# Projection stage: which engine empties PSUM into the scaled key and q tiles, the value pieces and the value rows

## The chip, the cores and the metric

The kernel runs on one core of a Trainium2 chip. The metric is the time of one execution on the device, in microseconds. Three runs of the kernel before gave 1306.35, 1302.48 and 1300.43 us, the median being 1302.48 us.

The engines are named as in the profile: PE is TensorE, DVE is VectorE, ACT is ScalarE, POOL is GpSimd, SP is the engine that issues the DMAs. PEld is the loading of weights into TensorE.

## The reference, cut to what matters

Two transformer-like layers with 256 tokens and 1024 columns come first, and a third block of another kind follows. Each of the first two layers projects the normalised input, and works on q, keys and values like this:

```python
proj = h @ w_in
q = proj[..., o0:o1].reshape(B, S, NSA_HEADS, HEAD_DIM)          # 8 heads of 64
kv = proj[..., o1:o2].reshape(B, S, 2, N_BRANCH, KV_GROUPS, HEAD_DIM)
q = rope(rms_norm(q, q_norm), pos)
k_s = rope(rms_norm(k_all[:, :, 1], k_norm[1]), pos)             # selected branch
k_w = rope(rms_norm(k_all[:, :, 2], k_norm[2]), pos)             # window branch
k_cmp = compress(k_all[:, :, 0], cmp_pe[0], cmp_w1[0], cmp_w2[0], blk)
v_cmp = compress(v_all[:, :, 0], cmp_pe[1], cmp_w1[1], cmp_w2[1], blk)
s = einsum(q, k) * scale                                          # scale = 1/8
# rms_norm(x, g) = x * rsqrt(mean(x*x) + EPS) * g
```

After that come softmax attention over three branches, a pooling mixer, an output projection and a feed-forward part.

## The kernel before, in words

Everything is written out by hand: one program per engine, ordered by semaphores. Each engine takes its instructions strictly in order, so the order of the lines in `pe_layer`, `act_layer` and `dve_layer` is the order of the work.

**Weights.** They arrive as panels of 1 MB (`raw`). For nearly full precision a panel is split in two: ACT rounds it into `w_hi` (`split_hi`, L409), DVE takes the rest into `ring_w` (`split_lo`, L414), and PE does three products for each tile (`mm3`, L419 to L421). SP loads the panels, and between them the modulation weights (`load_mod`, L348), each when its buffer is free.

**Modulation.** DVE also computes the vector-matrix products of the modulation, as multiply-adds over 128x512 tiles (`dve_mod`, L1115 for the first and L1117 for the others). These pieces are placed between its other work, as `mod(0)`, `mod(1)` and so on. `mod(3)` takes four L1117 instructions and needs the modulation weights that SP issued when `mod(1)` was done.

**Projection stage** (twice, once for each layer). PE fills banks 4 and 5 in turn, and a bank may be written again when `gfree` of that bank says that it has been emptied. The panels are, in order: K0K1, K2V0, V1V2, Q0, CMP (the hidden layer of the compression), then the gate columns, Q1, U0, U1. `turn(j)` on PE (L571 and L573) multiplies the squares of two tiles of keys or q by a block matrix of ones (the sums of squares) and the scaled tile `ybuf[j]` by a rotation matrix. For each j the rest is shared: ACT computes the reciprocal root in `roots(j)` (L953, L955), POOL multiplies `ybuf[j]` by the cosines (L429), DVE multiplies the rotated tile in PSUM by the sines (L1181), adds POOL's product (L1186) and multiplies by the root (L1188). The result goes to `kr` or `qr`. ACT copies it into the stacked operands (L1010, L979), and DVE computes what the copies rounded away (L1289, L1196). PE's first score products (`pe_maxima`, L828) wait for the last of these (`st_lo`, L824). The next thing that PE waits for is `cmp_y` (L655), set by DVE behind the gates and the compressed keys (L1302, L1303).

**What the change touches.** In the kernel before, DVE writes these tiles out of PSUM:

- `ybuf[0]`, the scaled keys, in two halves (L1247, L1262), 128x256 each;
- the V pieces of the compression, `tb`, in four parts (L1256), 64x240 each; ACT writes the K pieces (L962);
- the value rows `vt` (L1271), 128x512;
- `ybuf[1]` and `ybuf[2]`, the scaled q tiles (`scaled`, L1169), 128x512, multiplied by the norm's gain and by 0.125.

Of the kernel before, what the change touches and what calls it, by code (L numbers as in the profile page):

```python
# [9 lines left out]
ALU = mybir.AluOpType  # L10
ACT = mybir.ActivationFunctionType
# [4 lines left out]
T = 256  # L16
TT = T // P
# [3 lines left out]
EPS = 1e-6  # L21
# [17 lines left out]

C_ID, C_BD, C_ROT, C_ONE, C_COS, C_SIN, C_CCOS, C_CSIN, C_CAUS, C_CMPM, C_VALID, C_EPS, C_LEPS, C_MF, C_MB, C_SG, C_NM, C_RC, C_RM, CN = (  # L40
    0, 128, 256, 384, 512, 768, 1024, 1040, 1056, 1184, 1216, 1217, 1218, 1219, 1347, 1475, 1476, 1477, 2501, 2503)
N_CMP = (T - 32) // 16 + 1
# [19 lines left out]
def constants():  # L62
# [20 lines left out]
    c[:, C_EPS] = EPS  # L83
    c[:, C_LEPS] = LN_EPS
    c[:, C_MF:C_MF + P] = np.where(p > f, NEG, 0.0)
    c[:, C_MB:C_MB + P] = np.where(f > p, NEG, 0.0)
# [9 lines left out]
def build(nc, a, out, layers=DEPTH):  # L96
# [8 lines left out]
    with ctx:  # L105
# [299 lines left out]
        def split_hi(act, m, k):  # L405

            landed(act, m, k)
            act.wait_ge(split_free, 4 * m + k + 1)
            nc.scalar.activation(w_hi[slot(k)][:, :], w_raw(m, k), ACT.Copy).then_inc(hi_done, 1)  # L409

        def split_lo(dve, m, k):

            dve.wait_ge(hi_done, 4 * m + k + 1)
            nc.vector.tensor_tensor(w_lo(m, k), w_raw(m, k), w_hi[slot(k)][:, :].bitcast(F32),  # L414
                                    ALU.subtract).then_inc(lo_done, 1)
# [519 lines left out]
        def act_layer(act, l, link, ahead):  # L935
# [11 lines left out]
            def roots(j):  # L947


                act.wait_ge(nr_mm, 4 * l + (1, 2, 4)[j])  # L950
                i = (0, 2, 6)[j]
                v = tbuf[:, 2 * j:2 * j + 2, :]
                nc.scalar.activation(v, two(bank[i % 4][:, :]), ACT.Ln, bias=cst[:, C_EPS:C_EPS + 1], scale=1.0 / 64).then_inc(ring_a, 1)  # L953
                ring_taken(act, l, i)
                nc.scalar.activation(v, v, ACT.Exp, scale=-0.5).then_inc(nr_rs, 1)  # L955
# [3 lines left out]
            for g in range(2):  # L959
                for j2 in range(2):  # L960
                    src = win(G(0), 64 * g, 64, [[2, 16], [16, 15]], j2)
                    last = nc.scalar.activation(tb[64 * j2:64 * j2 + 64, :, 15 * g:15 * g + 15], src, ACT.Copy)  # L962
            last.then_inc(tb_k, 1)
            split_hi(act, m, 4)
            used(L_K2V0)
            nc.scalar.activation(tbuf[:, 1, :], G(1)[:, 0:T], ACT.Square).then_inc(nr_sq, 1)

            act.wait_ge(tb_pe, l + 1)
            nc.scalar.activation(tbh[:, :, :], tb, ACT.Copy).then_inc(tb_hi, 1)
            split_hi(act, m, 5)  # L970
            split_hi(act, m, 6)

            def stack(bp):
# [21 lines left out]
            used(L_Q0)  # L995
            nc.scalar.activation(tbuf[:, 2:4, :], two(G(3)[:, :]), ACT.Square).then_inc(nr_sq, 1)
            used(L_CMP)
            nc.scalar.activation(ce, bank[6][:, 0:60], ACT.Exp, scale=-1.0).then_inc(cmp_e, 1)
# [16 lines left out]
            used(L_Q1)  # L1015
            nc.scalar.activation(tbuf[:, 4:6, :], two(G(5)[:, :]), ACT.Square).then_inc(nr_sq, 1)
            act.wait_ge(nr_mm, 4 * l + 3)
            link(nc.scalar.activation(sqc[:, 16:31], bank[6][:, 256:271], ACT.Ln, bias=cst[:, C_EPS:C_EPS + 1], scale=1.0 / 64))
# [131 lines left out]
        def dve_layer(dve, l, link, ahead):  # L1150
# [13 lines left out]

            def scaled(j):


                dve.wait_ge(nr_sq, 5 * l + (3, 5)[j - 1])
                nc.vector.tensor_scalar(ybuf[j], two(G((3, 5)[j - 1])[:, :]), lc[:, LC_QN:LC_QN + 1], 0.125, ALU.mult, ALU.mult).then_inc(gfree[1], 1)  # L1169

            def rotated(j, parts=(0, 1)):
# [72 lines left out]

            used(L_K0K1)
            dve.wait_ge(tb_k, l + 1)
            nc.vector.tensor_scalar(ybuf[0][:, 0, :], G(0)[:, T:2 * T], lc[:, LC_KN + 1:LC_KN + 2], None, ALU.mult).then_inc(gfree[0], 1)  # L1247

            split_lo(dve, m, 4)
            used(L_K2V0)  # L1250

            dve.wait_ge(nr_sq, 5 * l + 2)
            for g in range(2):
                for j2 in range(2):
                    src = win(G(1), 64 * g, 64, [[2, 16], [16, 15]], T + j2)
                    last = nc.vector.tensor_copy(tb[64 * j2:64 * j2 + 64, :, 30 + 15 * g:45 + 15 * g], src)  # L1256
            last.then_inc(tb_v, 1)
            dve.wait_ge(tb_v, l + 1)
            pe_bc = win(lc, 0, P, [[2, 16], [1, 2], [0, 30]], LC_PE)
            tb4 = tb.rearrange("p j (v n) -> p j v n", v=2)  # L1260
            nc.vector.tensor_tensor(tb4, tb4, pe_bc, ALU.add).then_inc(tb_pe, 1)
            nc.vector.tensor_scalar(ybuf[0][:, 1, :], G(1)[:, 0:T], lc[:, LC_KN + 2:LC_KN + 3], None, ALU.mult).then_inc(gfree[1], 1)  # L1262
            nc.vector.memset(vt[:, :, :, 64:65], 1.0)
# [5 lines left out]
            split_lo(dve, m, 5)  # L1269
            used(L_V1V2)  # L1270
            nc.vector.tensor_copy(vt[:, :, :, 0:64], G(2)[:, :].rearrange("p (t s d) -> p t s d", t=TT, s=4)).then_inc(gfree[0], 1)  # L1271
            mod(1)
            split_lo(dve, m, 6)
            mod(2)

            scaled(1)
            dve.wait_ge(cmp_e, l + 1)
# [26 lines left out]
            split_lo(dve, m, 7)  # L1304
            scaled(2)
            maxima(0, (0, 1))
# [1145 lines left out]
```

## Time and profile before

| | |
|---|---|
| median of three runs | 1302.48 us |
| the profiled execution, own time | 1304.12 us |
| its span, first to last instruction | 1302.1 us |
| PE busy | 1214.6 us, 93% |
| DVE busy | 939.3 us, 72% |
| ACT busy | 608.3 us, 47% |
| chain that ended last | PE 70%, DVE 17%, DMA 7%, issue 3%, ACT 3% |
| mean granted clock of TensorE | 0.965 |

The span leaves out 2.0 us of the profiled execution's own time. "PEclk" is the clock that TensorE was granted, 1.00 being the level of 2.4 GHz and 0.5 that of 1.2 GHz. "Idle before" in square brackets is the time for which the engine stood still before an instruction, and which engine released it; "issue" means that the profile shows nobody for it. Starts are counted from the start of the span. The first layer's projection stage lies at about 46 to 112 us and the second layer's at about 388 to 454 us. Consecutive instructions of an engine overlap a little in the records, so that the distance between two starts says more than the duration.

### The profile page before, as it was taken

The numbers are of one execution on the slowest core, as the hardware profiler recorded it, in microseconds if no ns is written. First come the engines' busy times: TensorE is split into PE (matmuls) and PEld (weight loads), VectorE is DVE, ScalarE is ACT, GpSimd is POOL, SyncE is SP. The second block draws the span as 40 slices with busy tenths as digits, with TensorE's granted clock in tenths as the row PEclk, the third lists the DMA queues.
The fourth block names the chain that finished last, engine by engine and source line by source line (L and its number), as shares of the span: only waits on it lengthen the run. The fifth ranks groups of instructions, "written<-read, shape, count | busy, mean of one in ns | idle before, by whom it ended". The sixth has DMA issues, their size and how long they took to land.

```text
span 1302.1 us, 20323 instructions
## 1 busy us (share of the span) xinstructions
PE 1214.6 (93%) x8294; PEld 1103.9 (85%) x8294; DVE 939.3 (72%) x1211; ACT 608.3 (47%) x796; POOL 48.3 (4%) x54
## 2 busy tenths in 40 slices
PE   6799999999989999999999999998789999999996
PEld 5778889899889779899998998887669998788885
DVE  5798797786898986855657559987784647765565
ACT  2444344344344542544444435469685743444441
POOL 1003100000000140000000000000000000000000
PEclk7699999999999999999999999899989999999999
DMA  9772266667766422645556533255753463455540
GB/s 371 283 271 87 105 266 230 251 228 270 276 245 230 181 102 98 237 166 191 194 177 228 201 140 122 98 178 178 242 212 130 162 250 139 169 188 192 193 161 33
DMA packets 43804, 249.87 MB, mean 192 GB/s; under 512 B 4208, under 2 KB 12416, under 8 KB 15568
## 3 DMA queue, kind: packets, MB, share of 16 engines
q1 hardware_dynamic: 43280, 246.66, 52.0%
q0 software_dynamic: 448, 2.12, 0.4%
q8 instruction: 56, 0.92, 0.3%
q14 instruction: 20, 0.16, 0.0%
HBM read 247.66 MB, written 1.11 MB: 191 GB/s over the span
## 4 chain that ended last, share of the span: by engine, by line
PE 70%; DVE 17%; DMA 7%; issue 3%; ACT 3%; SPq 0%; DVEq 0%; ACTq 0%
PE bank L419 14%; PE bank L420 14%; PE bank L421 14%; PE bank L770 11%; DMA arena<-in_modw 5%; PE bank L771 5%; DVE ring_w L414 3%; DVE macc L1117 3%; PE bank L859 2%; DVE arena L1117 2%; DVE arena L2051 1%; PE bank L900 1%; DMA arena<-dscr 1%; PE bank L541 1%; PE bank L752 1%
## 5 line engine op out<-in xcount | busy, mean ns | idle before, releaser
L414 DVE TENSOR_TENSOR ring_w<-raw,w_hi 128x2048 fp32r<-128x2048 f32 x170 | 389.6, 2294 | 157.6 <-ACT w_hi L409 157.0
L409 ACT ACTIVATE w_hi<-raw 128x2048 fp32r<-128x2048 f32 x170 | 323.9, 1909 | 140.1 <-PE bank L421 121.5
L770 PE MATMUL bank<-act,w_hi 128*128 128x512 f32 x736 | 262.0, 398 | 6.2 <-DVE arena L1419 6.0
L419 PE MATMUL bank<-act,w_hi 128*128 128x256 f32 x800 | 237.3, 297 | 8.4 <-DVE act L1147 7.0
L420 PE MATMUL bank<-act,w_hi 128*128 128x256 f32 x800 | 231.1, 289 | 0.0
L421 PE MATMUL bank<-act,ring_w 128*128 128x256 f32 x800 | 230.9, 289 | 0.0
L771 PE MATMUL bank<-act,ring_w 128*128 128x256 f32 x736 | 206.2, 280 | 0.0
L419 PEld LDWEIGHTS bank<-act,w_hi 128*128 128x128 f32 x800 | 158.5, 198 | 17.0 <-issue 16.8
L770 PEld LDWEIGHTS bank<-act,w_hi 128*128 128x128 f32 x736 | 138.4, 188 | 39.6 <-DVE arena L1419 7.2
L419 PE MATMUL bank<-ff_hi,w_hi 128*128 128x256 f32 (+1 forms) x560 | 158.5, 283 | 1.0 <-issue 1.0
L420 PE MATMUL bank<-ff_lo,w_hi 128*128 128x256 f32 (+1 forms) x560 | 158.8, 283 | 0.0
L420 PEld LDWEIGHTS bank<-act,w_hi 128*128 128x128 f32 x800 | 158.6, 198 | 0.1
L421 PE MATMUL bank<-ff_hi,ring_w 128*128 128x256 f32 (+1 forms) x560 | 158.7, 283 | 0.0
L421 PEld LDWEIGHTS bank<-act,ring_w 128*128 128x128 f32 x800 | 158.3, 198 | 0.0
L771 PEld LDWEIGHTS bank<-act,ring_w 128*128 128x128 f32 x736 | 139.2, 189 | 0.5
L419 PEld LDWEIGHTS bank<-ff_hi,w_hi 128*128 128x128 f32 x560 | 107.4, 192 | 2.4 <-issue 1.1
L1068 ACT ACTIVATE arena<-bank 128x256 f32<-128x256 f32 x96 | 36.6, 383 | 154.7 <-PE bank L771 150.1
L421 PEld LDWEIGHTS bank<-ff_hi,ring_w 128*128 128x128 f32 x560 | 107.5, 192 | 0.0
L420 PEld LDWEIGHTS bank<-ff_lo,w_hi 128*128 128x128 f32 x560 | 107.5, 192 | 0.0
L1117 DVE SCALAR_TENSOR_TENSOR macc<-arena,cact,macc 128x512 f32<-128x512 f32 x105 | 82.5, 785 | 3.3
L1419 DVE TENSOR_TENSOR arena<-bank,arena 128x256 f32<-128x256 f32 x96 | 38.5, 419 | 45.9 <-ACT arena L1068 45.9
L1075 ACT ACTIVATE ff_hi<-arena 128x512 fp32r<-128x512 f32 x48 | 30.0, 626 | 64.6 <-DVE arena L1422 64.6
(337 smaller groups left out, 1957.5 us busy)
## 6 DMA issues: line engine op xcount, KB each, us to landing
raw<-in_panels SPq DMA_DIRECT2D x170, 1024.0 KB, 4.9
arena<-in_modw SPq DMA_DIRECT2D x48, 1024.0 KB, 6.7
mixf<-dscr SPq DMA_DIRECT2D x8, 512.0 KB, 4.4
arena<-dscr SPq DMA_DIRECT2D x8, 512.0 KB, 5.4
mixf<-dscr SPq DMA_DIRECT2D x8, 256.0 KB, 5.8
arena<-dscr SPq DMA_DIRECT2D x8, 256.0 KB, 6.7
arena<-in_lnr SPq DMA_DIRECT2D x1, 2048.0 KB, 9.2
cst<-in_cst SPq DMA_DIRECT2D x1, 1251.5 KB, 7.8
```

What stands on the lines that cost most here:

```text
L409: nc.scalar.activation(w_hi[slot(k)][:, :], w_raw(m, k), ACT.Copy).then_inc(hi_done, 1)
L414: nc.vector.tensor_tensor(w_lo(m, k), w_raw(m, k), w_hi[slot(k)][:, :].bitcast(F32), ALU.subtract).then_inc(lo_done, 1)
L419: nc.tensor.matmul(o, wh, xh, start=start, stop=False, skip_group_check=skip)
L420: nc.tensor.matmul(o, wh, xl, start=False, stop=False, skip_group_check=skip)
L421: return nc.tensor.matmul(o, wl, xh, start=False, stop=stop, skip_group_check=skip)
L770: nc.tensor.matmul(bank[4 + c][:, :], wh[:, s:s + P], act2[:, kc, :, :], start=kc == 0, stop=False)
L771: last = nc.tensor.matmul(bank[4 + c][:, 0:T], wl[:, s:s + P], act_hi[:, kc, :], start=False, stop=kc == KC - 1)
L859: mm = lambda o, w, x, first=False, last=False: nc.tensor.matmul(o, w, x, start=first, stop=last, skip_group_check=True)
L1068: nc.scalar.activation(fr[par][:, c * T:(c + 1) * T], up_bank(at, c, final)[:, T:2 * T], ACT.Copy).then_inc(ff_cross, 1)
L1075: nc.scalar.activation(ff_hi[:, par, :], fr[par], ACT.Copy).then_inc(ff_his, 1)
L1117: ins = nc.vector.scalar_tensor_tensor(o, src, c, o, ALU.mult, ALU.add)
L1419: nc.vector.tensor_tensor(fr[par][:, c * T:(c + 1) * T], up_bank(at, c, final)[:, 0:T], fr[par][:, c * T:(c + 1) * T], ALU.add).then_inc(f ...
```

## The change

ACT now writes the tiles out of PSUM that are named above, and DVE's instructions for them are gone. ACT applies the gain as its per-partition scale. The factor 0.125 of q goes into the reciprocal root: for q (`j` of 1 and 2) the logarithm is taken of the plain sum of squares plus 64 times EPS instead of the mean plus EPS, and the constants get one more column for that. In ACT's program the new instructions stand directly behind the one that squares the same bank. The core of the diff (... marks what is left out):

```diff
+    c[:, C_QEPS] = 64 * EPS
...
-                nc.scalar.activation(v, two(bank[i % 4][:, :]), ACT.Ln, bias=cst[:, C_EPS:C_EPS + 1], scale=1.0 / 64).then_inc(ring_a, 1)
+                eps, scale = (cst[:, C_QEPS:C_QEPS + 1], 1.0) if j else (cst[:, C_EPS:C_EPS + 1], 1.0 / 64)
+                nc.scalar.activation(v, two(bank[i % 4][:, :]), ACT.Ln, bias=eps, scale=scale).then_inc(ring_a, 1)
...
             last.then_inc(tb_k, 1)
+            nc.scalar.activation(ybuf[0][:, 0, :], G(0)[:, T:2 * T], ACT.Copy, scale=lc[:, LC_KN + 1:LC_KN + 2]).then_inc(gfree[0], 1)
             split_hi(act, m, 4)
             used(L_K2V0)
             nc.scalar.activation(tbuf[:, 1, :], G(1)[:, 0:T], ACT.Square).then_inc(nr_sq, 1)
+            for g in range(2):
+                for j2 in range(2):
+                    src = win(G(1), 64 * g, 64, [[2, 16], [16, 15]], T + j2)
+                    last = nc.scalar.activation(tb[64 * j2:64 * j2 + 64, :, 30 + 15 * g:45 + 15 * g], src, ACT.Copy)
+            last.then_inc(tb_v, 1)
+            nc.scalar.activation(ybuf[0][:, 1, :], G(1)[:, 0:T], ACT.Copy, scale=lc[:, LC_KN + 2:LC_KN + 3]).then_inc(gfree[1], 1)
...
             split_hi(act, m, 5)
+            used(L_V1V2)
+            nc.scalar.activation(vt[:, :, :, 0:64], G(2)[:, :].rearrange("p (t s d) -> p t s d", t=TT, s=4), ACT.Copy).then_inc(gfree[0], 1)
             split_hi(act, m, 6)
+            def scaled(j):
+                nc.scalar.activation(ybuf[j], two(G((3, 5)[j - 1])[:, :]), ACT.Copy, scale=lc[:, LC_QN:LC_QN + 1]).then_inc(gfree[1], 1)
...
             nc.scalar.activation(tbuf[:, 2:4, :], two(G(3)[:, :]), ACT.Square).then_inc(nr_sq, 1)
+            scaled(1)
...
             nc.scalar.activation(tbuf[:, 4:6, :], two(G(5)[:, :]), ACT.Square).then_inc(nr_sq, 1)
+            scaled(2)
```

On DVE the lines L1247, L1256 and L1262 and the waits in front of them are gone, and so are L1271 and both calls of `scaled` (L1276, L1305). `split_lo(dve, m, 4)` now stands directly in front of the wait for `tb_k`, and DVE waits for `tb_v` from ACT before it adds the position terms (L1261).

## Rows read from the trace of the kernel before

**Rows 1.** TensorE's waits, whole run: buffer, line, releaser: total us, times, longest.

```profile
PE bank L828 <- issue: 5.4, 2, 2.7
...
PE bank L896 <- DVE mix_lo L1338: 2.0, 2, 1.0
...
PE bank L656 <- DVEq L1303: 1.0, 2, 0.5
```

**Rows 2.** Chain that ended last, in order of time: start us, us, what.

```profile
81.37 0.66 DVE arena L1169
...
94.58 0.69 DVE stacks L1196
...
97.67 0.21 PE bank L419
...
102.63 0.23 PE bank L832
...
447.24 0.12 PE bank L419
```

**Rows 3.** VectorE in order of time, first layer: start us, us, instructions, idle before.

```profile
62.46 1.66 DVE L1256 COPY arena<-bank 64x240 f32<-64x240 f32 x4 [0.18 <-ACT arena L966]
...
72.70 0.68 DVE L1271 COPY arena<-bank 128x512 f32<-128x512 f32 x1
73.31 3.10 DVE L1117 SCALAR_TENSOR_TENSOR arena<-arena,cact 128x512 f32<-128x512 f32 x4
...
82.86 4.91 DVE L1117 SCALAR_TENSOR_TENSOR macc<-arena,cact,macc 128x512 f32<-128x512 f32 x4
87.69 0.68 DVE L1181 TENSOR_TENSOR arena<-bank,cst 128x512 f32<-128x512 f32 x1
88.41 0.69 DVE L1186 TENSOR_TENSOR arena<-arena 128x512 f32<-128x512 f32 x1
```

**Rows 4.** ScalarE in order of time, first layer.

```profile
56.49 1.52 ACT L962 ACTIVATE arena<-bank 64x240 f32<-64x240 f32 x4
...
61.97 0.39 ACT L966 ACTIVATE arena<-bank 128x256 f32<-128x256 f32 x1 [2.02 <-PE bank L421]
...
77.16 0.60 ACT L996 ACTIVATE arena<-bank 128x512 f32<-128x512 f32 x1 [7.19 <-PE bank L421]
...
89.86 2.60 ACT L1010 ACTIVATE stacks<-arena 64x512 fp32r<-64x512 f32 x4 [3.42 <-DVE arena L1188]
```

**Rows 5.** TensorE in order of time, first layer.

```profile
81.36 1.02 PE L571 MATMUL bank<-arena,cst 128*128 128x512 f32 x2
...
83.07 1.02 PE L571 MATMUL bank<-arena,cst 128*128 128x512 f32 x2
...
95.36 0.35 PE L828 MATMUL bank<-stacks 128*128 128x256 f32 x1 [2.69 <-issue]
```

**Rows 6.** GpSimd in order of time, first layer.

```profile
83.33 1.41 POOL L429 TENSOR_TENSOR arena<-arena,cst 128x512 f32<-128x512 f32 x1 [68.66 <-PE bank L573]
85.03 1.40 POOL L429 TENSOR_TENSOR arena<-arena,cst 128x512 f32<-128x512 f32 x1 [0.30 <-PE bank L573]
102.71 1.30 POOL L429 TENSOR_TENSOR arena<-arena,cst 128x512 f32<-128x512 f32 x1 [16.28 <-PE bank L573]
```

**Rows 7.** Stretches: us, then busy time and count by engine, PEclk, DMA share, GB/s.

```profile
97.60:102.00 4.40, 4.40 (x16) 3.23 (x16) 4.28 (x9) 0.49 (x2) 0.00 (x0) 0.61 0.00 0
145.20:152.00 6.80, 6.80 (x55) 6.42 (x55) 3.64 (x10) 1.64 (x1) 0.00 (x0) 1.00 0.33 136
439.00:442.60 3.60, 3.60 (x17) 3.60 (x18) 3.60 (x4) 0.49 (x2) 0.00 (x0) 0.53 0.00 0
814.00:826.00 12.00, 9.98 (x42) 8.66 (x43) 11.69 (x23) 3.80 (x6) 0.00 (x0) 0.57 0.18 77
```

**Rows 8.** DMA issues, near 76.5 and near 81.4 us: size, us to landing.

```profile
arena<-in_modw SPq DMA_DIRECT2D x1, 1024.0 KB, 5.7
...
arena<-in_modw SPq DMA_DIRECT2D x1, 1024.0 KB, 6.0
```

More of the change, by code:

```diff
@@ L37 @@
 LC_BM, LC_BA, LC_NA, LC_N2, LC_PS, LC_QN, LC_KN, LC_PE, LC_W2, LC_PW, LC_GW, LC = 0, 32, 48, 56, 64, 68, 69, 72, 104, 168, 680, 872
-C_ID, C_BD, C_ROT, C_ONE, C_COS, C_SIN, C_CCOS, C_CSIN, C_CAUS, C_CMPM, C_VALID, C_EPS, C_LEPS, C_MF, C_MB, C_SG, C_NM, C_RC, C_RM, CN = (
-    0, 128, 256, 384, 512, 768, 1024, 1040, 1056, 1184, 1216, 1217, 1218, 1219, 1347, 1475, 1476, 1477, 2501, 2503)
+C_ID, C_BD, C_ROT, C_ONE, C_COS, C_SIN, C_CCOS, C_CSIN, C_CAUS, C_CMPM, C_VALID, C_EPS, C_LEPS, C_MF, C_MB, C_SG, C_NM, C_RC, C_RM, C_QEPS, CN = (
+    0, 128, 256, 384, 512, 768, 1024, 1040, 1056, 1184, 1216, 1217, 1218, 1219, 1347, 1475, 1476, 1477, 2501, 2503, 2504)
 N_CMP = (T - 32) // 16 + 1
@@ L1163, in mod @@
                     dve_mod(dve, pair, maccs[(n + 1) % 2], turn % 2)
-            def scaled(j):
-                dve.wait_ge(nr_sq, 5 * l + (3, 5)[j - 1])
-                nc.vector.tensor_scalar(ybuf[j], two(G((3, 5)[j - 1])[:, :]), lc[:, LC_QN:LC_QN + 1], 0.125, ALU.mult, ALU.mult).then_inc(gfree[1], 1)
             def rotated(j, parts=(0, 1)):
@@ L1243, in dve_layer @@
                 dve_modc(dve, modc_ready, 3 * l + 2, 64, lc[:, LC_BM:LC_BM + 8], 12 * l + 5)
-            used(L_K0K1)
+            split_lo(dve, m, 4)
             dve.wait_ge(tb_k, l + 1)
[L1247 to L1257, printed above, removed]
             dve.wait_ge(tb_v, l + 1)
@@ L1261, in dve_layer @@
             nc.vector.tensor_tensor(tb4, tb4, pe_bc, ALU.add).then_inc(tb_pe, 1)
-            nc.vector.tensor_scalar(ybuf[0][:, 1, :], G(1)[:, 0:T], lc[:, LC_KN + 2:LC_KN + 3], None, ALU.mult).then_inc(gfree[1], 1)
             nc.vector.memset(vt[:, :, :, 64:65], 1.0)
@@ L1269, in dve_layer @@
             split_lo(dve, m, 5)
-            used(L_V1V2)
-            nc.vector.tensor_copy(vt[:, :, :, 0:64], G(2)[:, :].rearrange("p (t s d) -> p t s d", t=TT, s=4)).then_inc(gfree[0], 1)
             mod(1)
@@ L1274, in dve_layer @@
             mod(2)
-            scaled(1)
             dve.wait_ge(cmp_e, l + 1)
@@ L1304, in dve_layer @@
             split_lo(dve, m, 7)
-            scaled(2)
             maxima(0, (0, 1))
```

## The prediction

> **What bounds the kernel now.** I read the waits of TensorE first. The run has three waits in the layers' projection stage that the change can reach or that lie next to it, each once per layer: 2.7 us before the first score product (L828), 0.5 us before L656, and 1.0 us before L896, which comes much later and hangs on the pooling, not on the moved tiles [rows 1]. For L828 the view names no releaser, so the chain that ended last has to say who it is. Its piece before is VectorE's L1196 of 94.58 + 0.69 = 95.27 us, and TensorE starts L828 at 95.36 after standing still for 2.69 us [rows 2, 5]. So in this stage VectorE is late and TensorE waits for it. VectorE's instructions in order of time show why: from 62.46 on they follow each other almost without idle time [rows 3], while ScalarE stands still for 7.19 us before L996 and for 3.42 us before L1010 [rows 4]. An instruction taken from VectorE before 95 us is therefore on the path, as far as nothing else holds VectorE, and one given to ScalarE lies in a hole.
>
> The last view is the granted clock. After the two waits it is 0.61 in 97.60:102.00 and 0.53 in 439.00:442.60, that is, at the level of 1.2 GHz for most of the time [rows 7]. A product of L419 then takes 0.21 us in the chain, against 0.12 at full clock [rows 2].
>
> **Part by part.** Times are those of the first layer; I take the second as a copy, since the waits are equal.
>
> 1. V pieces and keys. VectorE begins the V pieces at 62.46, behind ScalarE's square at 61.97, and needs 1.66 us: until 64.12 [rows 3, 4]. On ScalarE the same shape takes 1.52 us for four. They can begin about 0.3 us after the square (the square's 0.39 us less the overlap of neighbouring records), at 62.25, so they end at 63.77, and VectorE adds the position terms at about 63.87: 0.3 us gained. The two writes of scaled keys cost nothing on either engine. The first goes to ScalarE, between its K pieces and the split of panel 4, and delays that split by at most 0.39 us, the row of this size; VectorE is then done with its half well before 63.8. The second lies beside the addition, for which ScalarE has to wait anyway. Were that cover gone, it would be 0.39 us.
> 2. Value rows. VectorE's L1271 goes; from its start to the next it is 73.31 - 72.70 = 0.61 us [rows 3]. ScalarE takes 0.60 us for a square of 128x512 [rows 4], between its splits of panels 5 and 6, in the hole before L996. No cost.
> 3. Scaled q for j = 1. VectorE's L1169 goes: its piece of the chain, from 81.37, is 0.66 us [rows 2]. On ScalarE it follows the square at 77.16 and ends at about 78.4, and `turn(1)` needs it after 81.36 [rows 4, 5]. No cost.
> 4. Sum so far: `mod(3)` starts 0.3 + 0.61 + 0.66 = 1.57 us earlier, at 81.3 instead of 82.86.
> 5. GpSimd. The four instructions of `mod(3)` take 4.91 us, whereas four of the same line at 73.31 take 3.10 [rows 3]. Between them lie GpSimd's two rope products at 83.33 and 85.03 [rows 6]. L1117 has two operands in SBUF. Of the four, two are slowed, and the whole costs 1.8 us. L1181, with one operand in PSUM, takes 0.68 us at 87.69 beside no GpSimd work, and the third rope product takes only 1.30 us against 1.4 [rows 3, 6]. My estimate from these: an L1117 that meets a rope product begins when that one is over, at about 84.74, and needs 0.55 us more. GpSimd's starts stay where they are, since TensorE sets them. Now three of the four instructions (0.79 us from start to start) fit before that, the fourth is held until 85.3 and L1181 follows. L1186 has two operands in SBUF again and is held by the second product until 86.43, so it ends at 87.0 instead of 88.41 + 0.69 = 89.1. The lead grows from 1.57 to 2.1 us. The bounds are 0.85 (below) and 3.2 (no collision left: 1.57 + 1.8, less a little). I take 2.1, as the one that follows from the rows in order of time.
> 6. Up to the wait. The copies of L1010 (2.60 us) and all behind them hang on this result on both engines [rows 4]; they move as a whole. L828 can start 2.1 us earlier, at 93.3. Of 2.69 us of idle, 0.6 stay. TensorE is next late for L656, as before by 0.5, since both sides of that wait move together.
> 7. The clock. The two waits were 3.2 us together and would be 1.1. The other wait, of 1.0 us before L896, is followed by a granted clock of 1.00 in 145.20:152.00 [rows 1, 7]. So I expect no fall here. What that gives: from L419 at 97.67 the chain needs 102.63 - 97.67 = 4.96 us up to L832 [rows 2]. At full clock it is 12 products of 0.12 = 1.44 us and two turn products. `turn(0)` has the same two at full clock, and the next L571 starts 83.07 - 81.36 = 1.71 us after its first [rows 5]. 4.96 - 1.44 - 1.71 = 1.8 us gained. The bounds are 0 (the clock falls all the same) and 2.0, with L656 and L657 in it.
> 8. Scaled q for j = 2, L1305. It goes from behind the wait. TensorE sets the pace there, so I count nothing. The third rope product, however, now starts near 98.8 instead of 102.71 [rows 6] and meets VectorE's small products of the compressed keys instead of L1181. They are held by up to 1.3 us, the duration of the product, of which the next TensorE step lets 0.2 us through. Cost 0.2, bounds 0 and 1.3.
> 9. The factor 0.125 in the root changes no instruction count. One more column of constants is 512 bytes. Both are nothing.
>
> Sum for each layer: 2.1 + 1.8 - 0.2 = 3.7 us, and twice that 7.3 us (rounded down). Behind the stage TensorE is busy for 6.80 of 6.80 us in the stretch of rows 7, so nothing there should give the gain back. The profiled execution of 1304.12 us (span 1302.1 and 2.0 around it) would become 1296.8. The median shown is 1.6 us lower than that execution, so the forecast is 1302.48 - 7.3 = **1295.2 us**.
>
> The Trainium skill has the rule behind step 5 in "SBUF — State Buffer", section "SBUF: two separate sides": VectorE with two SBUF inputs and GpSimd share a pair of ports under an exclusive lock, and the loser waits for the whole instruction. By it the added lead is bound to the order of the two engines, as in the case "lock" below. The trace agrees, with 4.91 us for the four L1117 against 3.10.
>
> **Rivals.**
>
> - *Lock.* `mod(3)` cannot start before its weights land. The request of 76.44 would go out at about 75.5 and took 5.7 us, the next one 6.0 [rows 8]: 81.2 to 81.5, right at the 81.3 where VectorE is ready. If it comes 0.5 us late, GpSimd's product at 83.33 goes ahead of the third L1117; this and the fourth are each held, and L1181 starts at 86.85 instead of 87.69. The lead is then 0.85 us and the wait 1.9 us. With the clock kept: 2 x (0.85 + 1.8 - 0.2) = 4.9, so 1297.6 us. For it speaks how close 81.3 and 81.5 are; against it, that the earlier request has less in flight beside it.
> - *Clock.* The stall shrinks, but the clock falls as before: 2 x (2.1 - 0.2) = 3.8 us, so 1298.7 us. For it speaks that two waits lie close together; against it, L896.
> - *All of it.* GpSimd doesn't hold L1186 and both waits nearly vanish: 2 x (3.2 + 1.8) = 10.0 us, so 1292.5 us.
> - *Hidden.* ScalarE or a transfer takes VectorE's place before L828 (the L1010 copies, say, released later than I think): no stall is removed, 1302.5 us. Against it: ScalarE's 3.42 us of idle before L1010.
> - *Slower.* The clock falls and stays down for longer. In 814.00:826.00 it was granted 0.57, so 12 x 0.43 / 0.5 = 10.3 us at the lower level, against 4.4 x 0.39 / 0.5 = 3.4 here [rows 7]. Each us at that level loses (0.21 - 0.12) / 0.21 = 0.43 us. 6.9 us more cost 3.0 us, and less the lead of 1.9 this is 1.1 per layer: 1304.7 us. It decides from 4.4 us of longer fall. For it speaks only that the stage now ends its stall in another pattern; against it, that TensorE is fully busy behind it.
>
> **How the numbers follow.** Forecast 0.5, lock 0.18, clock 0.15, all of it 0.06, hidden 0.06, slower 0.05. The range takes in all but part of the last two, with about 2 us for the spread of the three runs (1300.43 to 1306.35): 1290 to 1302 us. A change of 0.5% is 6.5 us, about what a measurement can tell from none. The forecast's 7.3 is just above it, so I give it three quarters of its chance (0.38); with "all of it" and a part of the lock case for larger effects elsewhere it makes 0.5 for faster. Slower is 0.04, the rest 0.46.
>
> **What would show each step.** In the changed profile: L1261 0.3 us earlier; `mod(3)` near 81.3 with one slow L1117 instead of two; L1186 long (near 1.1 us) and ending near 87.0; L828 with 0.6 us of idle in front; 1.00 as the granted clock up to 102 us and in the second layer alike; ScalarE busier by about 3 us per layer in all with no PE wait on it. I am wrong if the two L1117 still take over 4.5 us, if `mod(3)` waits for a DMA, if the clock falls to 0.6 again, or if a new wait of TensorE on ScalarE or behind 102 us takes the gain.

## The result, and the profile of the changed kernel

| | before | changed |
|---|---|---|
| median of 20 runs each, same chips | 1303.2 us | 1294.66 us |
| lowest to highest | 1297.69 to 1307.72 | 1289.27 to 1305.63 |
| profiled execution | 1304.12 us | 1296.6 us |
| its span, mean granted clock | 1302.1 us, 0.965 | 1294.4 us, 0.967 |

The ratio of the changed kernel to the one before is 0.9936, with a 95% interval of 0.9919 to 0.9952: 6.3 to 10.6 us faster, 8.3 at the centre. The forecast was 1295.2 us. Whether each step came about as told is another question: one step was wrong, and the size given to another was too large.

First, the page of the changed kernel: busy time by engine, the TensorE clock and the shares of the chain that ended last.

```profile
span 1294.4 us, 20322 instructions
PE 1211.3 (94%) x8294; PEld 1100.0 (85%) x8294; DVE 929.7 (72%) x1193; ACT 615.8 (48%) x814; POOL 48.1 (4%) x54
PEclk7699999999999999999999999899989999999999
PE 72%; DVE 15%; DMA 7%; ACT 3%; issue 2%; SPq 0%; DVEq 0%; ACTq 0%
```

The page alone would not tell the reader much: nothing in it has the size of a cause. The waits of TensorE do. (In the changed kernel the lines have moved: L828 is L829, L656 is L657, L896 is L897, L571 and L573 are L572 and L574, L1117 is L1135, L1181 is L1193, L1186 is L1198, L1261 is L1263, L429 is L430.)

```profile
PE bank L829 <- issue: 2.5, 2, 1.8
...
PE bank L897 <- DVE mix_lo L1335: 2.0, 2, 1.0
...
PE bank L657 <- DVEq L1301: 0.5, 1, 0.5
```

The wait before the first score product was 5.4 us in all [rows 1] and is 2.5; its longest is 1.8. The one before L897 stayed, as told. Now VectorE in order of time, in the same stretch as [rows 3]:

```profile
63.36 1.16 DVE L1263 TENSOR_TENSOR arena<-arena,lc 128x960 f32<-128x960 f32 x1 [1.24 <-ACT arena L973]
...
71.90 3.11 DVE L1135 SCALAR_TENSOR_TENSOR arena<-arena,cact 128x512 f32<-128x512 f32 x4
...
81.28 5.09 DVE L1135 SCALAR_TENSOR_TENSOR macc<-arena,cact,macc 128x512 f32<-128x512 f32 x4 [0.39 <-DMA arena<-in_modw]
86.29 0.68 DVE L1193 TENSOR_TENSOR arena<-bank,cst 128x512 f32<-128x512 f32 x1
87.00 0.69 DVE L1198 TENSOR_TENSOR arena<-arena 128x512 f32<-128x512 f32 x1
```

`mod(3)` waits 0.39 us for its weights, its four instructions take 5.09 us instead of 3.11, and L1198 takes an undisturbed 0.69. That is the rival "lock" of the prediction, row by row. In the second layer of the same execution the weights are there in time, and the forecast's own pattern shows: one slow L1135 (4.00 us) and an L1198 held to 1.07 us.

```profile
420.85 4.00 DVE L1135 SCALAR_TENSOR_TENSOR macc<-arena,cact,macc 128x512 f32<-128x512 f32 x4
424.76 0.68 DVE L1193 TENSOR_TENSOR arena<-bank,cst 128x512 f32<-128x512 f32 x1
425.48 1.07 DVE L1198 TENSOR_TENSOR arena<-arena 128x512 f32<-128x512 f32 x1
```

ScalarE now does the moved work, in the holes that [rows 4] showed: the value pieces (L973), the scaled keys (L975), the value rows (L981) and the scaled q (L987).

```profile
61.74 1.52 ACT L973 ACTIVATE arena<-bank 64x240 f32<-64x240 f32 x4
63.28 0.47 ACT L975 ACTIVATE arena<-bank,lc 128x256 f32<-128x256 f32 x1
...
67.27 0.57 ACT L981 ACTIVATE arena<-bank 128x512 f32<-128x512 f32 x1
...
77.14 0.68 ACT L987 ACTIVATE arena<-bank,lc 128x512 f32<-128x512 f32 x1
```

TensorE and GpSimd in the same stretch, to set against [rows 5, 6]:

```profile
80.84 1.02 PE L572 MATMUL bank<-arena,cst 128*128 128x512 f32 x2
...
93.96 0.49 PE L829 MATMUL bank<-stacks 128*128 128x256 f32 x1 [1.82 <-issue]
```

```profile
82.81 1.27 POOL L430 TENSOR_TENSOR arena<-arena,cst 128x512 f32<-128x512 f32 x1 [68.19 <-PE bank L574]
84.52 1.30 POOL L430 TENSOR_TENSOR arena<-arena,cst 128x512 f32<-128x512 f32 x1 [0.44 <-PE bank L574]
```

And the granted clock in the stretches that answer to [rows 7]:

```profile
94.00:102.00 8.00, 8.00 (x29) 5.94 (x29) 5.65 (x15) 2.08 (x6) 0.00 (x0) 0.57 0.28 115
434.00:440.00 6.00, 5.50 (x22) 3.91 (x21) 4.60 (x11) 0.92 (x4) 0.00 (x0) 0.72 0.36 153
```

GpSimd's first product begins at 82.81, ahead of the third L1135 of the late `mod(3)`, and so VectorE is held twice. And in this one execution the clock still fell to the 1.2 GHz level, in the first layer for longer than before (0.57 over 8 us). The bare profile of the changed kernel looks like two rivals come true at once, "lock" and "clock", and yet the median of 20 runs is where the forecast had it. By the signs that the prediction gave for being wrong, three are there: four L1135 of over 4.5 us, a `mod(3)` that waits for a DMA, and a clock of 0.57. One profile was not enough to read a change of this size, so the study rests on more executions and on a measure that can be compared between them: the **stage length**, from the first product of `turn(0)` (L571, L572) to the first product of the pooling, with the offset of the first score product (L828, L829) inside it. The microseconds at the low clock are counted in the granted-clock record within the stage.

| profile | stage, layer 1 / 2 | to first score product | low clock in stage |
|---|---|---|---|
| before | 60.9 / 60.7 | 14.0 / 14.0 | 3.4 / 3.4 |
| before, again | 61.2 / 61.8 | 14.0 / 14.0 | 6.8 / 6.8 |
| changed | 60.7 / 58.7 | 13.1 / 11.9 | 6.8 / 3.4 |
| changed, again | 57.6 / 57.3 | 12.2 / 12.0 | 0 / 0 |
| changed, third | 57.5 / 57.3 | 12.1 / 11.9 | 0 / 0 |

The mean stage is 61.2 us before (4 stages) and 58.2 us in the changed kernel (6 stages). Twice the difference, 6.0 us, is most of the 8.3 us, but lies just under the lower end of its interval. In the first profile of the changed kernel the stages account for 0.2 + 2.0 us of the 7.7 us of span; 5.5 us lie outside them. There that execution has 10.7 us less at the low clock than the one before (73.9 against 84.6; for example 391 to 395 us before, without a counterpart after). At the 0.41 us that each cost in the stage, worked out below, this is an estimated 4.4 of the 5.5 us. Both kernels do the same work there, and the other profiles of the changed kernel have 98.1 and 81.1 us there, against 80.6 in the second one of the kernel before; so I do not put these falls down to the change.

### The profile page after: what moved, and what is told of

It reads as the page before. It is cut to its first block, busy times and chain, and to the rows that moved or that the text cites. A ratio compares the mean times of both kernels' runs of the same rounds, so it can differ in the third digit from the quotient of the medians.

```text
span 1294.4 us, 20322 instructions
## 1 busy us (share of the span) xinstructions
PE 1211.3 (94%) x8294; PEld 1100.0 (85%) x8294; DVE 929.7 (72%) x1193; ACT 615.8 (48%) x814; POOL 48.1 (4%) x54
## 4 chain that ended last, share of the span: by engine, by line
PE 72%; DVE 15%; DMA 7%; ACT 3%; issue 2%; SPq 0%; DVEq 0%; ACTq 0%
PE bank L420 14%; PE bank L421 14%; PE bank L422 14%; PE bank L771 11%; PE bank L772 5%; DMA arena<-in_modw 5%; DVE ring_w L415 3%; PE bank L860 2%; DVE macc L1135 2%; DVE arena L2048 1%; PE bank L901 1%; DVE arena L1135 1%; DMA arena<-dscr 1%; PE bank L542 1%; PE bank L753 1%
## 5 line engine op out<-in xcount | busy, mean ns | idle before, releaser
L1135 DVE SCALAR_TENSOR_TENSOR macc<-arena,cact,macc 128x512 f32<-128x512 f32 x105 | 81.7, 778 | 3.7 <-DMA arena<-in_modw 0.4
L1416 DVE TENSOR_TENSOR arena<-bank,arena 128x256 f32<-128x256 f32 x96 | 38.4, 418 | 46.5 <-ACT arena L1086 46.3
```

What stands on the lines that cost most here:

```text
L1135: ins = nc.vector.scalar_tensor_tensor(o, src, c, o, ALU.mult, ALU.add)
L1416: nc.vector.tensor_tensor(fr[par][:, c * T:(c + 1) * T], up_bank(at, c, final)[:, 0:T], fr[par][:, c * T:(c + 1) * T], ALU.add).then_inc(f ...
```

## The experiments

**Theory.** VectorE's lead up to L828 is the cause of the gain; all else (clock, GpSimd lock) follows from how early VectorE is. **Rivals.** The gain comes from the clock alone (TensorE's activity pattern); or from the order in which transfers land; or from the q tiles alone.

### Give VectorE the time back (pad)

The changed kernel with two useless maxima on VectorE per layer, of about 0.6 us from start to start.

```
+            pad = lambda: nc.vector.tensor_reduce(scr[:, :], cst[:, C_RC:C_RC + 2 * T]..., AX.X, ALU.max, negate=True)
             split_lo(dve, m, 5)
+            pad()
             mod(1)
             ...
             mod(2)
+            pad()
```

> The changed kernel with two idle VectorE instructions put back where two of the removed ones stood: a maximum over 512 columns (about 0.6 us each), in front of mod(1) and behind mod(2), 1.2 us per layer. ScalarE still writes all tiles and banks are emptied as early as in the changed kernel. Theory 'VectorE's time in front of L829 is what the change buys': the wait before L829 grows again, from 1.8 and 0.7 us to 2.3 to 2.9 us in both layers, and most of the gain goes: 3 to 7 us slower than the changed kernel, 1298 to 1302 us. Rival 'the gain comes from banks that are emptied earlier, or from elsewhere in the run': the wait stays below 2 us and the time stays at 1294 to 1296 us.

Measured: 1303.9 us, ratio to before 0.9999 (0.9985 to 1.0013). The stages are 62.2 / 62.1, the offset 13.9 / 13.9.

```profile
PE bank L830 <- issue: 5.2, 2, 2.6
```

```profile
80.97 5.14 DVE L1136 SCALAR_TENSOR_TENSOR macc<-arena,cact,macc 128x512 f32<-128x512 f32 x4
```

The wait came back as expected (2.6 us in both layers); the time is above the 1298 to 1302 us that I had given. 1.2 us more on VectorE, with everything else of the change in place, take away the whole gain. `mod(3)` begins 1.17 us behind `turn(0)` (79.80), against 1.50 before (82.86 - 81.36, [rows 3, 5]) and 0.03 earlier than `turn(0)` in the changed kernel's second layer (420.85, 420.88); the wait is back at 2.6 us. Moving work to ScalarE has no worth of its own here, where the clock falls in both stages (6.8 us each): only VectorE's lead has. At full clock this is not so, as q2_back will show.

### Only the scaled q tiles (q_only)

The kernel before, with `scaled(1)` and `scaled(2)` on ScalarE and the factor in the root; value pieces, keys and value rows stay on VectorE.

```
             nc.scalar.activation(tbuf[:, 2:4, :], two(G(3)[:, :]), ACT.Square).then_inc(nr_sq, 1)
+            scaled(1)
             ...
-            scaled(1)
             dve.wait_ge(cmp_e, l + 1)
```

> The kernel before with only the q part of the change: the scaled q tiles on ScalarE and 0.125 in the root; keys, V pieces and value rows stay on VectorE. Its lead in front of mod(3) is 0.66 us of the 1.57 worked out for the whole. Theory 'each us of VectorE in front of L828 counts once, plus what the lock and the clock add': mod(3) starts 0.6 to 0.7 us earlier, the wait before L828 is 1.7 to 2.3 us, and the time lies between the two kernels, 1298 to 1302 us. Rival 'the part behind the wait (the second q tile) carries the gain': 1294 to 1297 us with a wait of over 2 us.

Measured: 1301.33 us, 0.9974 (0.9959 to 0.9989). Offset 13.4 / 13.4, stages 60.2 / 61.6.

```profile
PE bank L829 <- issue: 4.2, 2, 2.1
```

```profile
80.36 4.91 DVE L1124 SCALAR_TENSOR_TENSOR macc<-arena,cact,macc 128x512 f32<-128x512 f32 x4
```

The first score product comes 0.6 us earlier for one L1169 of 0.66 us removed [rows 2], and the four `mod(3)` instructions still take 4.91 us. So this part is worth about 0.26% of 0.64%, and it takes the others to move `mod(3)` in front of GpSimd's products. That half of the effect depends on them together agrees with the lock; the intervals are too wide to prove a proportion.

### The same kernels again (before_again, after_again, after_third)

Nothing edited: the kernel before and the changed kernel, profiled anew.

> The kernel before once more, unchanged, for a second profile. Theory 'which stretches are run at the lower clock differs from execution to execution': the projection stages (from the first turn product to the pooling's products) take 60.9 and 60.7 us in the first profile; here they lie within 59.5 to 63 us, with the waits of 2.7 and 0.5 us as before, and stretches at the lower clock stand at partly other places of the run. Rival 'the clock falls at fixed places': stages within 0.3 us of the first profile and the same places.

> The changed kernel once more, unchanged, for a second profile. Theory as for the kernel before: mod(3) waits for its weights in the first layer again or is close to it, the wait before L829 is 1.5 to 1.9 us there and 0.6 to 0.9 in the second, but the stretches at the lower clock differ, so that the stages take 58.5 to 61.5 us. Rival 'fixed places': 60.8 and 58.7 us again.

> The changed kernel a third time, for a third profile. So far its stages took 60.8 and 58.7 us (mod(3) late by its weights and the clock fallen twice in the first layer, once in the second) and 57.6 and 57.3 us (clock 1.00). Theory 'the weights land close to the moment at which VectorE is ready, and either order is possible': each stage of this profile is near one of these cases, within 57 to 61 us, and where the four L1135 take over 4.9 us the wait before L829 is over 1.5 us.

Measured: 1302.95, 1299.98 and 1295.48 us (single runs); stages and offsets in the table above. For the changed kernel, again, I had expected stages of 58.5 to 61.5 us and a wait of 1.5 to 1.9 us in the first layer; both missed, since the good pattern held in both layers. The 1299.98 us execution has the short stages too (57.6 / 57.3): it loses its time elsewhere, with 98.1 us at the low clock in all against 81.1 in the third. From the changed kernel, again, VectorE:

```profile
81.35 4.00 DVE L1135 SCALAR_TENSOR_TENSOR macc<-arena,cact,macc 128x512 f32<-128x512 f32 x4 [0.18 <-DMA arena<-in_modw]
85.27 0.68 DVE L1193 TENSOR_TENSOR arena<-bank,cst 128x512 f32<-128x512 f32 x1
85.98 1.09 DVE L1198 TENSOR_TENSOR arena<-arena 128x512 f32<-128x512 f32 x1
...
99.03 1.25 DVE L1310 TENSOR_TENSOR kbd<-small,sqc 64x15 f32<-64x15 f32 x1
```

```profile
93.33 0.36 PE L829 MATMUL bank<-stacks 128*128 128x256 f32 x1 [0.92 <-issue]
```

```profile
83.08 3.44 POOL L430 TENSOR_TENSOR arena<-arena,cst 128x512 f32<-128x512 f32 x2 [68.56 <-PE bank L574]
98.96 1.29 POOL L430 TENSOR_TENSOR arena<-arena,cst 128x512 f32<-128x512 f32 x1 [12.44 <-PE bank L574]
```

The weights are 0.18 us late here and the good pattern still holds; at 0.39 us it did not, and neither at 0.36 us, in a later profile (q2_back):

```profile
80.29 5.09 DVE L1138 SCALAR_TENSOR_TENSOR macc<-arena,cact,macc 128x512 f32<-128x512 f32 x4 [0.36 <-DMA arena<-in_modw]
```

So the step from one case to the other lies between 0.18 and 0.36 us of lateness. The prediction had said 0.5.

### The transfer (load8)

In the queue of SyncE the load of panel 8 goes behind the weights of `mod(3)`.

```
             gate_mod(2)
-            load(sp, m, 8)
             gate_mod(3)
+            load(sp, m, 8)
```

> The changed kernel with the load of weight panel 8 issued behind the modulation weights of mod(3) instead of in front of them. In the changed kernel's trace mod(3) of the first layer waited 0.39 us for these weights, and GpSimd's products then met it as in the kernel before (5.09 us for four L1135, 1.8 us of wait at L829), while the second layer, without that wait, has 4.00 us and 0.7 us. Theory 'the late weights cost the first layer its lead, by way of the lock': no DMA wait, four L1135 in about 4.0 us, 0.6 to 0.9 us of wait at L829 in the first layer too; 1 to 3 us faster than the changed kernel. Rival 'the first layer differs for another cause': the wait stays at 1.8 us.

Measured: 1297.27 us, 0.9941 (0.9925 to 0.9957); the profiled execution has 1292.16 us and a span of 1290.0. Stages 57.3 / 57.3, offset 11.9 / 11.9, no low clock in them.

```profile
arena<-in_modw SPq DMA_DIRECT2D x1, 1024.0 KB, 4.8
```

```profile
78.25 4.00 DVE L1135 SCALAR_TENSOR_TENSOR macc<-arena,cact,macc 128x512 f32<-128x512 f32 x4
82.17 0.68 DVE L1193 TENSOR_TENSOR arena<-bank,cst 128x512 f32<-128x512 f32 x1
82.88 1.07 DVE L1198 TENSOR_TENSOR arena<-arena 128x512 f32<-128x512 f32 x1
```

```profile
PE bank L829 <- issue: 1.3, 2, 0.7
```

The weights land in 4.8 us instead of the 6.2 of the changed kernel's first layer, and no wait on them is left. `mod(3)` begins at 78.25 with `turn(0)` at 78.27. This is one profile, and two of the three profiles of the changed kernel are free of the "lock" case without the edit. What speaks for the transfer is its time: in the first layer the weights took 5.9 to 6.2 us to land in all five profiles with the old order (the changed kernel three times, fill_after, q2_back), and the "lock" case is there just where VectorE waited 0.36 us or more for them. In the median nothing of this is to be seen, though I had expected 1 to 3 us: load8 and the changed kernel have the same ratio within their intervals. The late weights cost 1.2 us of offset in one layer of some executions, and an interval is 0.003 wide, some 4 us.

### The clock (fill_after, fill_before)

Useless products of TensorE in the two waits, into a bank that nobody reads: 8 and 4 in the changed kernel, 16 and 4 in the kernel before. They keep TensorE busy where it waited.

```
+            for _ in range(16):
+                nc.tensor.matmul(bank[7][:, 64:64 + T], act_hi[:, 0, 0:P], act_hi[:, 1, :], start=True, stop=True)
             pe.wait_ge(masks_ready, 6)
             ...
+            for _ in range(4):
+                nc.tensor.matmul(...)
             pe.wait_ge(nr_sq, 5 * l + 4)
```

> The changed kernel with work of no use for TensorE: 8 products of 128x256 in front of the wait of L829 and 4 in front of the wait for the compressed keys (about 0.12 us each), into unused columns of bank 7. Theory 'the clock falls because TensorE stands still here, and the fall costs 1 to 2 us per layer': the granted clock stays at 1.00 through the stage in both layers, the stage of the first layer gets about 2.5 us shorter behind L829 and the whole 1 to 4 us faster. Rival 'the fall is not set by this idle time': the clock falls as before and the whole is 0 to 1 us slower, by the products that exceed the wait in the second layer.

> The kernel before with TensorE work of no use in its two waits (16 products of 128x256 in front of L828, 4 in front of the compressed keys); no tile is moved and VectorE's path is the same. It has the clock's part of the gain without VectorE's lead. Theory 'the fall of the clock is a cost of its own, of about 1.5 us for each 3.4 us at the lower level': the products L828 start 14.0 us behind the first turn product as before, but the clock stays at 1.00 and the stages take 58.8 to 59.5 us instead of 60.7 to 61.9; 1298 to 1302 us. Rival 'the clock's fall only goes with the wait and costs little': stages over 60 us and no gain.

Measured: fill_after 1294.68 us, 0.994 (0.9919 to 0.996), stages 58.5 / 57.3, offset 13.1 / 12.1 (the weights were late in the first layer: 0.41 us, four L1139 in 5.04). fill_before 1297.76 us, 0.9962 (0.9941 to 0.9983), stages 60.3 / 60.4, offset 14.0 / 14.0. In neither does the clock fall in the stage. fill_after's part behind L829 is 2.2 us shorter in the first layer than in the first profile of the changed kernel (2.5 expected), but the run as a whole has the same ratio as the changed kernel, where I had expected 1 to 4 us. For the kernel before I had expected stages of 58.8 to 59.5 us. They missed that, and the reason is in the waits of its TensorE and in VectorE's order there:

```profile
PE bank L571 <- issue: 1.8, 2, 0.9
...
PE bank L832 <- issue: 1.6, 2, 0.8
```

```profile
98.90 0.74 DVE L1173 TENSOR_SCALAR arena<-bank,lc 128x512 f32<-128x512 f32 x1
```

```profile
99.75 1.10 PE L571 MATMUL bank<-arena,cst 128*128 128x512 f32 x2 [0.90 <-issue]
```

At full clock TensorE reaches `turn(2)` before VectorE has written the second scaled q tile (L1173 here) and freed its bank: a wait of 0.9 us per layer that the slow clock had covered in the kernel before. The tile that I had costed at nothing was the next thing late. The run time of fill_before gained more than its stages: 5.0 us (2.2 to 7.8 by the interval) against twice 0.8. What that says of the profiles is taken up further down.

### The second q tile back on VectorE (q2_back)

fill_after, with `scaled(2)` moved back to VectorE. This tells apart what that tile is worth.

```
-            scaled(2)
             act.wait_ge(nr_mm, 4 * l + 3)
             ...
             split_lo(dve, m, 7)
+            dve.wait_ge(nr_sq, 5 * l + 5)
+            nc.vector.tensor_scalar(ybuf[2], two(G(5)[:, :]), lc[:, LC_QN:LC_QN + 1], None, ALU.mult).then_inc(gfree[1], 1)
```

> The changed kernel with TensorE's filler products, and the second scaled q tile back on VectorE (behind the low split of panel 7, as in the kernel before); all else on ScalarE. The clock is to stay at 1.00, so that only this tile differs from the filled changed kernel, whose stages take 45.3 to 45.4 us from the first score product to the pooling's. Theory 'the tile that lies behind the wait, which I had costed at nothing, holds up the last turn products once the clock is up': a wait of 0.7 to 1.1 us in front of them, and 46.2 to 46.5 us for that part in both layers; 1 to 3 us slower in all. Rival 'TensorE sets the pace there': 45.4 us again.

Measured: stages 59.4 / 58.3 against 58.5 / 57.3 of fill_after, at the same offsets (13.1 / 12.1): 0.9 us per layer, all behind L829.

```profile
97.69 1.10 PE L572 MATMUL bank<-arena,cst 128*128 128x512 f32 x2 [0.90 <-issue]
```

The run time, however, is 1294.81 us, 0.9941 (0.9918 to 0.9963), the same as fill_after's 0.994. Two such stages should cost 1.9 us, or 0.0014; I had expected 1 to 3 us. Each interval is 0.004 wide, so the run times neither show it nor speak against it; the stage does.

### `mod(3)` out of the way (late_after, late_before, late2)

In both kernels `mod(3)` goes behind the small products of the compressed keys, and the split of panel 7 behind it; in late2 `mod(3)` goes behind the second stack, panel 7 keeps its place, TensorE's `mod(1)` goes behind the score units of the first half, and VectorE's sum of the first modulation pair goes behind the split of panel 9.

```
-            mod(3)
             rotated(0)
             ...
-            split_lo(dve, m, 7)
             ...
+            mod(3)
             rotated(2, (0,))
             ...
+            split_lo(dve, m, 7)
             stack(1)
```

> The changed kernel with mod(3) taken out of VectorE's path to L829 (it now stands behind the small products of the compressed keys) and the low half of panel 7 split behind the seventh maximum. Theory 'VectorE is late only by what stands in front of L829': no wait before L829 and none before the products of the compressed keys, clock 1.00 through the stage in both layers, two slow L1135 gone from this place; 4 to 8 us faster than the changed kernel, 1287 to 1291 us. Rival 'another releaser (the ScalarE copies L1027, or GpSimd's products) stands close behind': a wait of over 1 us stays and the gain is under 2 us.

> The kernel before with the same move of mod(3) and of the low split of panel 7, none of the changed kernel's tiles moved to ScalarE. Theory 'the change buys nothing but VectorE's lead over L829': with mod(3) out of the way that lead is there anyway, the wait before L828 is under 0.3 us, and the time is that of the changed kernel with the same move within 1.5 us. Rival 'the moved tiles are worth something of their own (less VectorE work in all, earlier free banks)': 3 us or more slower than that kernel.

> The changed kernel with mod(3) further back than in the first attempt: on VectorE behind the second stack, on TensorE mod(1) behind the first seven score units, and the sum of the first pair behind the split of panel 9. The first attempt took 58.0 us for a stage because three new waits came up (0.6 at L833, 0.5 at the first U1 product, 0.5 for the compressed keys). Theory 'VectorE has room only behind the second stack': no wait before L829 and none at L833, stages of 56.0 to 57.0 us against 57.3 for the changed kernel without a fall of the clock; 1289 to 1294 us. Rival 'the work comes due again at the score units or the maxima of the second half': stages of 57.3 us or more and no gain over the changed kernel.

| | median, ratio (95%) | stages | offset |
|---|---|---|---|
| late_before | 1298.59, 0.9961 (0.9942 to 0.9981) | 58.7 / 58.7 | 11.3 / 11.3 |
| late_after | 1296.34, 0.9952 (0.9927 to 0.9976) | 58.1 / 58.1 | 11.3 / 11.3 |
| late2 | 1294.58, 0.9923 (0.9904 to 0.9942) | 57.7 / 57.5 | 11.3 / 11.3 |

With `mod(3)` gone from in front of `rotated(0)`, the offset is the same with and without the change. VectorE now waits for TensorE (late_after):

```profile
80.27 0.69 DVE L1193 TENSOR_TENSOR arena<-bank,cst 128x512 f32<-128x512 f32 x1 [1.85 <-PE bank L574]
81.69 0.69 DVE L1198 TENSOR_TENSOR arena<-arena 128x512 f32<-128x512 f32 x1 [0.73 <-POOL arena L430]
```

Where VectorE is not late, its lead is worth nothing up to L828, and what is left of the change is 0.7 us behind it, near what q2_back gives for the second q tile. By the ratios the two kernels are 1.2 us apart (1.5 by the theory, 3 or more by the rival), with intervals that overlap widely. Moving `mod(3)` and the split alone in the kernel before shortens the stage by 2.4 us (61.17 - 58.74), without any work taken off VectorE. Part of this is the clock, which does not fall in these stages: against fill_before, where it does not either, the move gives 1.6 us. My forecast of 1287 to 1291 us for late_after missed: TensorE has new waits behind L829. late_before shows them in the same form, in the first two rows here; in late_after these two are 1.2 and 1.1 us. The wait of L656 was there before.

```profile
PE bank L832 <- DVE arena L1181: 2.5, 2, 1.3
...
PE bank L419 <- DVE ring_w L414: 1.1, 2, 0.5
PE bank L656 <- DVEq L1302: 1.0, 2, 0.5
```

`mod(3)` (4.03 us) is merely late at the next place: part of it was pushed behind L828, not taken away. late2 missed too: I had expected stages of 56.0 to 57.0 us, and TensorE still waits 0.6 us at L833 in the first layer, for VectorE's maxima. late2 has the lowest ratio of all, but 0.9923 (0.9904 to 0.9942) and the changed kernel's 0.9936 (0.9919 to 0.9952) overlap: not shown to be better.

## Why the prediction was right, and where it was not

- **Steps 1 to 4, the start of `mod(3)`: right.** It was to begin 1.57 us earlier. Against `turn(0)` it began 1.50 us behind before, and 0.03 us ahead in the second layer and 0.02 ahead in load8: 1.53 and 1.52 us. The position terms (L1263) start 1.9 us behind ScalarE's square (63.36 - 61.46), before it was 64.16 - 61.97 = 2.2: the 0.3 us of step 1.
- **Step 5, the lock: right where the weights are in time.** One slow `mod(3)` instruction instead of two (4.00 us instead of 4.91), L1198 held (1.07 to 1.09 us), lead 14.0 - 11.9 = 2.1 us as forecast. Where they are late it was the rival "lock", close to both of its numbers: lead 14.0 - 13.1 = 0.9 us (0.85 told), 1.82 us of wait (1.9 told). Of the five profiles with these transfers (three of the changed kernel, fill_after, q2_back) three have it in the first layer and none in the second. The Trainium skill's rule in "SBUF — State Buffer", section "SBUF: two separate sides" (the loser waits for the whole instruction), agrees: in the changed kernel, again, L1198 ends at 87.07, 0.55 us behind GpSimd's second product (83.08 + 3.44 = 86.52), and even the tiny L1310 of 64x15, whose neighbours take 0.17 us, is held for 1.25 us, the length of GpSimd's third product (1.29 us).
- **Step 6, the wait: right.** 2.69 us of idle were to become 0.6; measured 0.63 to 0.66 in the good case (load8, twice; the changed kernel's second layer, three times), 0.92 with the weights 0.18 us late. The 0.5 us at L656 stayed.
- **Step 7, the clock: mis-sized.** I put 1.8 us of gain behind L828 down to the clock. What lies behind L828 is 46.9 / 46.7 and 47.2 / 47.8 us long before and 45.4 us where the changed kernel keeps its clock, so 1.3 to 2.4 us came. But with the clock kept and the old code (fill_before) it is 46.3 in both layers (fill_after's 45.4 / 45.2 show that the useless products behind L828 add nothing): the clock alone is 0.4 to 1.4 us of it, depending on the execution, and 0.4 to 0.6 in the very execution that the prediction was read from. The price of a microsecond at the low level was right where nothing else holds TensorE: the changed kernel's second layer, with 3.4 us of it, is 58.7 - 57.3 = 1.4 us longer, 0.41 each (0.43 told). What failed is that full clock for TensorE doesn't make the stage as much shorter as TensorE is faster, since `turn(2)` then waits for VectorE.
- **Step 8, the second q tile: wrong.** I costed it at nothing plus a loss of 0.2. It is a gain of 0.9 us per layer where the clock is full, shown by q2_back against fill_after, where nothing else differs. fill_before's wait of 0.9 us and the 0.7 us between late_before and late_after agree. The failed step is my sentence that TensorE sets the pace there: it did at the low clock of [rows 7], and it was wrong to carry that over to the full clock that step 7 assumed. The stages show that it did: with 3.4 us at the low clock the part behind L828 is 46.9 and 46.7 us before and 46.8 in the changed kernel, so there the moved tile is worth nothing. The collision of the third rope product did come (L1310), with no visible cost.
- **The sum.** Steps 7 and 8 are off in opposite directions, and the sum of 3.7 us per layer is 61.17 - 57.43 = 3.7 in the stages of the good case. That the sum fits is in part luck: the prediction had no ground for the 0.9 us that fill what step 7 has too much. (Twice 3.7 is 7.4; the 7.3 there is a slip of no weight.)
- **The chances.** "Lock" and "clock" were treated as whole-run cases. They are cases of one layer of one execution. The clock fell in 2 of the changed kernel's 6 stages, against 4 of 4 before, 2 of 2 in pad and 2 of 2 in q_only. So a median lies between the cases.
- **Why the run times gain more than the mean stages.** The stages give 6.0 us, the run times 8.3 (6.3 to 10.6); in fill_before it is 1.6 against 5.0, and in q_only 0.6 against 3.4. The granted clock of each run tells part of it. (1 - clock) x 2 x span is the time at the low level: in the mean 96 us in 76 executions of the kernel before, and 81 us in 20 of the changed kernel. The 15 us between them, at 0.41 each, are an estimated 6 us of the 9.1 us between the mean spans. The profiled stages show only 6.8 us less per execution (10.2 before, 3.4 changed). By this estimate the clock has the larger part of the gain in the run times, more than the half that the prediction gave it, and the few profiles show too little of it. Where the other 8 us at the low level lie, no profile shows.

## What to carry to other kernels

When a term of the sum rests on a stall or a slow clock going away, cost every other part of the change in the state that this term creates, not in the state of the old trace: the tile that was worth nothing beside a slow TensorE was worth 0.9 us beside a fast one. Moving work off the late engine counts only as lead in front of the next wait. Before taking work away, look at what merely stands in front of the late chain: moving `mod(3)` and one split behind it gave 2.4 us per layer here (0.8 of it by the clock that no longer fell), the whole change 3.0 (3.7 where the clock did not fall). Below 1%, compare the length of the one stage over several profiles, together with the medians; one pair of profiles puts clock falls elsewhere down to the change. Compare the mean clock of all runs too; it showed here what five profiles did not.

## What the runs showed of the hardware that I had not expected

**The clock falls in another pattern each time.** The same changed kernel has 84.2, 98.1 and 81.1 us at the low level in three profiles, the kernel before 91.5 and 94.3. In the stage, idle times of 0.64 to 0.92 us before L829 were followed by no fall in the two later profiles, while 0.63 us in the second layer of the first one was (434 to 440 us, 0.72). The idle time before the score products alone does not decide it.

**Once in a while TensorE is granted the low level over a long stretch in which it is fully busy.** It is in the profiles of three kernels, late_after, late2 and q2_back:

```profile
478.00:504.00 26.00, 26.00 (x124) 24.76 (x124) 11.36 (x22) 2.87 (x3) 0.00 (x0) 0.54 0.05 14
```

```profile
142.00:168.00 26.00, 26.00 (x124) 24.76 (x124) 11.51 (x22) 2.56 (x3) 0.00 (x0) 0.54 0.22 74
```

```profile
144.00:170.00 26.00, 26.00 (x124) 24.76 (x124) 11.26 (x21) 2.19 (x2) 0.00 (x0) 0.54 0.21 76
```

TensorE is busy for 26.00 of 26.00 us and gets 0.54. The executions with it took 1308.41, 1308.34 and 1302.51 us, up to 14 us above the medians of their kernels. All three lie at the same place of the program: they begin about 2 us behind the wait of 0.98 us before the pooling (here late2's; it is at 476.99 in late_after and at 142.16 in q2_back).

```profile
140.67 0.48 PE L897 MATMUL bank<-vca,act_flat 32*128 32x130 f32 x2 [0.98 <-DVE mix_lo L1335]
```

The wait is the same in the kernel before (0.98 at 145.14), whose clock there is 1.00 [rows 7], and in every other stage. My argument against the rival "clock", that the 1.0 us wait before L896 leaves the clock alone, is true only most times: 3 of the 28 stages profiled have a long fall behind it. What decides it is open, and whether the long fall goes when this wait does was not tried.

**Prices of the moved writes.** ScalarE's copy with a scale operand takes 0.47 us for 128x256 and 0.68 for 128x512 from PSUM. Without one, its square of 128x256 takes 0.39, its copy of the value rows 0.57 and its square of 128x512 0.60: 0.08 to 0.11 us less. VectorE's same tile took 0.74. The move is free because ScalarE had a hole, and it would be nearly so by duration as well.
